# Outputs of a pair of heads issued inside the fourth unit, one small product behind each main matmul

## The reference

```python
def step(S, inp):
    ...
    scores = jnp.where(causal, jnp.einsum('bthk,bshk->bhts', q_dec, k_dec), 0.0)
    o = jnp.einsum('bthk,bhkv->bthv', q_dec, S) + jnp.einsum('bhts,bshv->bthv', scores, vc)
    S = jnp.exp(b_last)[..., None] * S + jnp.einsum('bshk,bshv->bhkv', k_end, vc)
    return S, o
```

## Time and profile before

| | before |
|---|---|
| median of 3 runs | 1232.63 us (1231.08 to 1233.11) |
| the profiled execution | 1232.07 us, span 1230.3 us |
| mean granted TensorE clock | 0.991 of full |
| TensorE matmuls | 1190.3 us, 97% of the span, 8108 instructions |
| TensorE weight loads | 1146.0 us, 93% |
| VectorE | 652.7 us, 53% |
| ScalarE | 580.7 us, 47% |
| GpSimd | 764.5 us, 62% |
| outputs of the pairs | 336 instructions of TensorE, in 8 blocks of 42 |

### The profile page before, as it was taken

The page is one execution under the profiler, slowest core; times in us unless marked ns, Lnnn a source line. Parts: engine busy times, 40 slices in busy tenths (PEclk is TensorE's granted clock), DMA queues, the critical chain, the costliest instruction groups (busy, mean ns, idle before and its releaser), DMA issues.

```text
span 1230.3 us, 23529 instructions
## 1 busy us (share of the span) xinstructions
PE 1190.3 (97%) x8108; PEld 1146.0 (93%) x8108; DVE 652.7 (53%) x1251; ACT 580.7 (47%) x964; POOL 764.5 (62%) x592
## 2 busy tenths in 40 slices
PE   5999999999999999999999999999999999999995
PEld 4897899999999999999989879999999999999995
DVE  5355367763776652255162643867468565405533
ACT  6574334443446664344355633443443566524532
POOL 3664546554777777777775554555557767777772
PEclk9999999999999999999999999999999999999998
DMA  7754534443544445444566554434444444444451
GB/s 267 255 186 156 172 123 156 140 123 103 189 138 150 142 152 154 146 146 153 159 210 203 189 194 148 153 109 123 140 129 146 148 143 151 146 148 153 149 152 57
DMA packets 53207, 190.72 MB, mean 155 GB/s; under 512 B 6032, under 2 KB 7312, under 8 KB 52880
## 3 DMA queue, kind: packets, MB, share of 16 engines
q1 hardware_dynamic: 43632, 159.15, 41.4%
q10 hardware_dynamic: 9504, 30.56, 6.6%
HBM read 181.15 MB, written 8.53 MB: 154 GB/s over the span
## 4 chain that ended last, share of the span: by engine, by line
PE 88%; DVE 6%; DMA 2%; issue 2%; ACT 1%; POOL 1%; SPq 0%; DVEq 0%; ACTq 0%; POOLq 0%
PE bank L1070 44%; PE bank L1101 28%; PE bank L1112 6%; DMA raw<-w 2%; PE bank L1306 1%; PE bank L1283 1%; PE bank L1327 1%; PE bank L1324 1%; DVE arena L679 1%; DVE arena L769 1%; POOL wlo L251 1%; DVE arena L946 1%; PE bank L1195 1%; PE bank L1184 1%; ACT whi L286 1%
## 5 line engine op out<-in xcount | busy, mean ns | idle before, releaser
L251 POOL TENSOR_TENSOR wlo<-raw,whi 128x512 fp32r<-128x512 f32 x588 | 764.3, 1321 | 446.9 <-PE bank L1101 233.9
L286 ACT ACTIVATE whi<-raw 128x1024 fp32r<-128x1024 f32 x294 | 310.7, 1057 | 287.6 <-PE bank L1070 167.1
L1101 PE MATMUL bank<-oh,whi 128*128 128x320 f32 x848 | 269.9, 318 | 3.8 <-DVE arena L964 2.1
L1101 PE MATMUL bank<-ol,whi 128*128 128x320 f32 x848 | 264.7, 312 | 0.0
L1101 PE MATMUL bank<-oh,wlo 128*128 128x320 f32 x848 | 264.6, 312 | 0.0
L1070 PE MATMUL bank<-hh,whi 128*128 128x320 f32 x832 | 257.8, 310 | 0.4 <-DVE hl L956 0.4
L1070 PE MATMUL bank<-hl,whi 128*128 128x320 f32 x832 | 257.1, 309 | 0.0
L1070 PE MATMUL bank<-hh,wlo 128*128 128x320 f32 x832 | 257.1, 309 | 0.0
L1101 PEld LDWEIGHTS bank<-oh,whi 128*128 128x128 f32 x848 | 161.8, 191 | 9.4 <-issue 3.7
L1101 PEld LDWEIGHTS bank<-ol,whi 128*128 128x128 f32 x848 | 161.7, 191 | 0.3
L1101 PEld LDWEIGHTS bank<-oh,wlo 128*128 128x128 f32 x848 | 161.5, 190 | 0.0
(11 more groups left out here) (195 smaller groups left out, 1536.2 us busy)
## 6 DMA issues: line engine op xcount, KB each, us to landing
raw<-w SPq DMA_DIRECT2D x296, 512.0 KB, 3.6
arena<-cache_k ACTq DMA_DIRECT2D x16, 512.0 KB, 5.9
arena<-cache_v ACTq DMA_DIRECT2D x16, 512.0 KB, 5.2
arena<-st_in ACTq DMA_DIRECT2D x8, 512.0 KB, 5.6
sst_out<-arena ACTq DMA_DIRECT2D x8, 512.0 KB, 3.2
con<-consts SPq DMA_DIRECT2D x1, 1288.0 KB, 13.6
x<-x_in SPq DMA_DIRECT2D x2, 640.0 KB, 10.6
arena<-mem_in SPq DMA_DIRECT2D x2, 512.0 KB, 6.5
```

What stands on the lines that cost most here:

```text
L251: i = pool.tensor_tensor(out=wlo[:, s % 2, h], in0=raw[:, s, h], in1=whi[:, s, h].bitcast(f32), op=ALU.subtract)
L286: nc.scalar.activation(whi[:, s, :], raw[:, s, :], ACT.Copy).then_inc(hi_ready, 1)
L1101: r = MM(o, a, b[:, k, 0:n], start=k == 0 and i == 0, stop=k == KT_ - 1 and i == 2, skip_group_check=True)
```

## The change

`outputs(p)` becomes `output(p, i)`, which issues the i-th of the 21 products, and `unit` gets an argument `small`, which it calls behind each main matmul. The block behind the fourth unit goes; its three waits stand ahead of the fourth unit, and the products come one behind each of that unit's first 21 main matmuls (so main, and two instructions of a small product, in turn). Of two loops the nesting differs: the products of the masked scores go over heads inside, not outside. `o_done` is signalled by the 21st product, three main matmuls ahead of the unit's end. No other engine's list changes.

```diff
-            def unit(u, xh, xl, n, first_wait=None):
+            def unit(u, xh, xl, n, first_wait=None, small=None):
...
                     for i, (a, b) in enumerate(((wh, xh), (wh, xl), (wl, xh))):
                         r = MM(o, a, b[:, k, 0:n], start=k == 0 and i == 0, stop=k == KT_ - 1 and i == 2, skip_group_check=True)
+                        if small is not None and k * 3 + i < 23:
+                            small(k * 3 + i)
                 r.then_inc(unit_done, 1)
...
-                def gated(u):
-                    unit(u, oh, ol, T)
+                def gated(u, small=None):
+                    unit(u, oh, ol, T, small=small)
...
+                def output(p, i):
+
+                    if i < 6:
+                        e, a = i % 2, i // 2
...
+                    elif i < 6 + NCH - 1:
+                        c = i - 5
                         MM(heads(C[0][:, :])[:, :, c * CHUNK:(c + 1) * CHUNK], S[:, c - 1, :], qz[:, :, c * CHUNK:(c + 1) * CHUNK],
                            start=False, stop=c == NCH - 1, skip_group_check=True)
-                    for b in range(DEC_BATCH):
+                    elif i < 6 + NCH - 1 + DEC_BATCH:
+                        b = i - 6 - NCH + 1
                         r = MM(heads(C[1][:, 0:2 * NS])[:, :, 8 * b:8 * b + 8], s0[:, p % 2, b, :], qz[:, :, SEQ + 8 * b:SEQ + 8 * b + 8],
                                start=False, stop=b == 7, skip_group_check=True)
-                    r.then_inc(o_done, 1)
+                        if b == 7:
+                            r.then_inc(o_done, 1)
...
                     gated(u + 1)
                     gated(u + 2)
-                    gated(u + 3)
                     pe.wait_ge(s_ready, lv * 8 + 2 * p + 2)
                     pe.wait_ge(st_s[p % 2], lv * 32 + 16 * (1 + p // 2))
                     pe.wait_ge(scm_ready, lv * 16 + 4 * p + 4)
-                    outputs(p)
+                    gated(u + 3, lambda i: output(p, i))
                     gated(u + 4)
```

More of the change, by code:

```diff
@@ L1308, in sample_updates @@
                     r.then_inc(us_done, 1)
[L1310 to L1318, removed]
-                        h = 2 * (p % 2) + e
[L1320 to L1323, removed]
+                def output(p, i):
+                    if i < 6:
+                        e, a = i % 2, i // 2
+                        h = 2 * (p % 2) + e
+                        if a < 2:
+                            o, t0 = C[0][:, e * SEQ + a * P:e * SEQ + (a + 1) * P], e * SEQ + a * P
+                            MM(o, vt[:, p // 2, a, h * P:(h + 1) * P], scm[:, t0:t0 + P], start=i == 0, stop=False, skip_group_check=True)
+                        else:
+                            t0 = 2 * SEQ + e * NS
+                            MM(C[1][:, e * NS:(e + 1) * NS], vt[:, p // 2, 2, h * P:(h + 1) * P], scm[:, t0:t0 + NS], start=e == 0, stop=False,
+                               skip_group_check=True)
+                    elif i < 6 + NCH - 1:
+                        c = i - 5
                         MM(heads(C[0][:, :])[:, :, c * CHUNK:(c + 1) * CHUNK], S[:, c - 1, :], qz[:, :, c * CHUNK:(c + 1) * CHUNK],
                            start=False, stop=c == NCH - 1, skip_group_check=True)
-                    for b in range(DEC_BATCH):
+                    elif i < 6 + NCH - 1 + DEC_BATCH:
+                        b = i - 6 - NCH + 1
                         r = MM(heads(C[1][:, 0:2 * NS])[:, :, 8 * b:8 * b + 8], s0[:, p % 2, b, :], qz[:, :, SEQ + 8 * b:SEQ + 8 * b + 8],
                                start=False, stop=b == 7, skip_group_check=True)
-                    r.then_inc(o_done, 1)
+                        if b == 7:
+                            r.then_inc(o_done, 1)
                 pe.wait_ge(qz_zero, 2)
```

## The result

| | before | after |
|---|---|---|
| median, same chip | 1232.87 us (4 runs, 1231.08 to 1234.46) | 1248.44 us (4 runs, 1248.23 to 1249.83) |
| ratio, 95% interval | | 1.0129, 1.0112 to 1.0147 |
| span of the profiled execution | 1230.3 us | 1246.5 us |
| waits for VectorE's state updates | 0.2 us (TensorE's weight load) | 17.5 us (TensorE's matmuls; 18.0 its weight loads) |

A forecast was written before the change was run, and what follows sets the result against it. The prediction took TensorE's instruction stream, with the few places where it waits, as the bound (88% of the chain). Its terms, -4.6 + 16.1 + 2.8 = +14.3 us on 1232.1, gave 1246.4 us, range 1238 to 1251.

The forecast's parts named there:

- 1. The stream: TensorE's mixed units: alternating main and small products costs the sum of the block's prices, 0.369 us a step; change 0.
- Rival A: TensorE's mixed units: weight loads run further ahead in alternation, 6.0 us less, 1240.4 us; chance 8%.
- rival D: TensorE's mixed units: small products' loads take no time behind main matmuls, so faster than before, 1226.2 us; chance 5%.
- 2. The clock in the new units: Mixed units: wide operands between small products remove three clock falls of 1.55 us, -4.6 us.
- Rival C: Mixed units: the clock falls there all the same, the three falls stay, 1251.0 us; chance 9%.
- 3. The waits ahead of the fourth unit: TensorE's waits for states, masked scores and loaded state, moved one unit ahead, stay covered; cost 0.
- 4. The late unit_done: First pair, each layer: later signal delays silu(3) and VectorE's chain, stalling TensorE; 8.7 plus 7.4 us, together 16.1.
- Rival B: VectorE's batch keys and query copies, first pairs: no port conflict with GpSimd, 16.1 falls to 7.9, 1238.2 us; chance 10%.
- 5. The clock behind the waits: Behind TensorE's two stalls: the clock falls, 1.4 us each, +2.8 us, bounds 0 and 3.1.

The follow-up runs named there:

- Experiment 6: No alternation, first-pair silu(3) behind the padded queries: on the kernel before 1231.95 us; with the 21 products as a block ahead of the fourth unit 1231.93 us.
- experiments 4 and 5: Changed kernel with the padded query copies on ScalarE (4), 1243.55 us; with the first pair's batch keys ahead of silu(3) (5), 1242.12 us.
- experiment 3: Changed kernel without alternation, the 21 products as a block ahead of the fourth unit: 1251.90 us, ratio 1.0161.
- experiment 2: Changed kernel with the old order (fourth unit, then the block) for the first pair of each layer: 1227.88 us, ratio 0.9963.

## Why the prediction was right, point by point

**1. The stream: 0, right.** In the second pair of layer 0, five units and the 42 small instructions lie between the end of the sample updates and the sum of squares. Before, 201.01 to 223.29, 22.28 us. After, the chain has

```profile
209.66 7.18 PE bank L1101 x49
...
231.96 0.86 PE bank L1360 x2
```

231.96 - 209.66 = 22.30 us: 0.02 us for a whole mixed unit, 0.001 us for a product. In the chain the pieces of a mixed unit recur every 0.37 us (here the first pair of layer 0), as the sum of the prices said:

```profile
174.11 0.24 PE bank L1101
174.48 0.24 PE bank L1101
174.85 0.24 PE bank L1101
```

Rival A (0.33 us a step) and rival D are out. The weight loads show why, in the same unit:

```profile
173.19 0.19 PEld L1101 LDWEIGHTS bank<-ol,whi 128*128 128x128 f32 x1
173.30 0.34 PEld L1330 LDWEIGHTS bank<-qz,arena 128*128 128x128 f32 x2
```

The main matmul starts at 173.22 and one load of the small product beside it, at 173.30. The two loads end at 173.64 and one takes 0.19, so the second starts at 173.45, with the small product's first pass and not ahead of it. One load runs ahead and no more; what alternation hides under a main matmul, the block hid as well.

**2. The clock in the new units: -4.6 us, right.** Three falls behind blocks went beside the one of the first pair, and none came in the mixed units. In the third pair of layer 0, for one, the way from the end of the sample updates to the next chunk updates took 276.12 - 239.59 = 36.53 us before and 283.25 - 248.25 = 35.00 after. Experiment 6 shows no other gain of alternation. Rival C is out. That three blocks of the profiled execution would have been followed by a fall is what its trace said, and how many another execution has isn't on record.

**3. The waits ahead of the fourth unit: 0, right.** No row of the table of waits has them.

**4. The late unit_done: 16.1 us, measured 16.0.** From the end of the sample updates to line 1360: layer 0 before 184.72 - 160.90 = 23.8, after 191.56 - 160.50 = 31.1, so 7.2 us (7.4 said); layer 1 before 782.18 - 759.89 = 22.3, after 796.91 - 765.90 = 31.0, so 8.7 (8.7 said). The batch keys (2.1 said, 3.39 - 1.29 = 2.1 measured) and the copies (2.0 said, 2.58 - 0.68 = 1.9) came out each for itself, and experiments 4 and 5 took each out for its length. The price of the copies came from a copy of 8 columns (line 807) and held for one of 320, so what is paid there is a wait, not a rate. Rival B is out.

**5. The clock behind the waits: 2.8 us, measured 4.6, the term that was mis-sized.** The two sums of squares cost 2.50 - 1.08 = 1.42 us more in each layer and the three units behind them 10.94 - 10.56 = 0.38 and 11.95 - 10.56 = 1.39 us: 1.8 and 2.8 us. The bound of 3.1 us was two falls at the price of a fall behind a block. Behind a standstill of 8.8 us that price is no bound. The table by stretches shows how far the low level reached into the work, first in layer 0, then in layer 1:

```profile
191.60:194.80 3.20, 3.20 (x8) 2.17 (x9) 0.94 (x2) 0.70 (x2) 0.00 (x0) 0.50 0.00 0
...
796.90:802.30 5.40, 5.39 (x16) 4.36 (x17) 3.13 (x3) 2.23 (x3) 0.00 (x0) 0.50 0.24 97
```

From 194.9 and from 802.5 on it is 1.00. Half of these 3.2 and 5.4 us is lost, 1.6 and 2.7 for the 1.8 and 2.8 measured. Why the clock came back 2 us later in layer 1, behind a wait of the same length, the runs don't settle. The prediction was right that a part of the fall passes while TensorE is idle, but what was left for the work cost as much as a fall behind a block, or nearly twice as much.

The sum with the measured terms is 16.0 - 4.6 + 4.6 = 16.0 us, and the spans differ by 16.2. Of the rest, 0.6 us is the wait for line 679, which was 6.7 us before and 7.3 after, in a part the change doesn't touch; with that the sum is 0.4 us over, and the wait at the start is 0.3 us shorter (9.9 and 9.6). By the medians the time came out 2.0 us above the forecast, and 1.8 of them are term 5.

## What to carry to other kernels

When work is folded into another piece, that piece's completion signal moves behind it: list who waits for that signal, and what stands behind the waiting instruction in that engine's order. Here a gain of about 5 us was covered by a loss of 22 us that one instruction, placed ahead of steps that didn't need it, let through to TensorE. And on TensorE, mixing narrow products with wide ones saved nothing in the stream, but it kept the clock up: the gain is to be looked for in the granted clock, not in the spacing.

## What the runs showed of the hardware that I hadn't expected

TensorE can be busy for 100% of a stretch and still have its clock lowered. Behind the blocks of narrow float32 products it fell in four, three and four of eight cases (the kernel before and the two of experiment 6), in two of eight in experiment 3 and in none of two in experiment 2. Where the same products alternated with 320-column ones, it fell in none of 38 cases in five kernels. Which trait of the mixed order keeps it up, the wide operands between or the longer steps, no run separates.

And an instruction of VectorE that meets GpSimd can lengthen by about 1 us, somewhat less than one of GpSimd's (1.3 us and more), whatever its own size: copies of 64x320 went from 0.34 to 1.28 us each, batch keys of 64x512 from 0.65 to 1.70, and of the chunk keys of 128x256, which take 0.41 each as a rule, the longest in the kernel before took 1.52. It depends on the moment (both batch keys together took 2.59 us in experiment 5 and 3.39 in the changed kernel). The state updates with an operand in PSUM kept their 0.36.
